# Features on partitions: conv inputs, memory queries and tile 1's gate and up without turns, with the norm's factor spread

## The chip, the cores and the metric

The kernel runs on one core of a Trainium2 chip, in one launch. The metric is the device time of that launch in microseconds. TensorE (PE in the profile) multiplies, VectorE (DVE) and ScalarE (ACT) work element by element, GpSimd (POOL) issues the gathers, SyncE (SP) issues the weight transfers. All numbers are 32-bit floats. A matmul of 32-bit operands stands in the trace as two records, each with its own weight load; a turn (a transpose through PE against the identity) is one record.

## The reference, cut to what matters

There are 256 tokens of 1024 features. A first block (retention and differential attention, then a feed-forward that gathers 128 experts for each token) ends in x; a second block of two layers runs on it. What the change touches is in the second block:

```python
h = rms_norm_2(x, norm_mix[0])                     # x * rsqrt(mean(x*x) + eps) * g
b_gate, c_gate, u = jnp.split(h @ w_in, 3, axis=-1)       # short_conv_mixer, 1024 x 3072
z = c_gate * u
conv = causal depthwise convolution of z over 3 tokens
x = x + (b_gate * conv) @ w_out

q = rms_norm_2(x, norm_mem[l]) @ w_q               # mem_cross_attention, both layers
s = einsum(q, k) * 256 ** -0.5; p = softmax(s)
x = x + merge(p @ v) @ w_o

g, u = jnp.split(rms_norm_2(x, norm_ffn[l]) @ w_gu, 2, axis=-1)   # swiglu, 1024 x 5632
x = x + (jax.nn.silu(g) * u) @ w_down
```

## The kernel before, in words

**Tiles and units.** The tokens are two tiles of 128 (tile 0 and tile 1). A product of the second block is cut into units: one unit is 1024 input features by 512 output columns (a 2 MB piece of weights), or 128 tokens by 512 columns of output, and fills one PSUM bank. Four banks (`bank[u % 4]`) go round in the order of the list `UNITS`; a unit opens when the unit four before it has been read by its engine (D for DVE, A for ACT). `layer_unit` (L954 to L965) does one with eight matmuls of 128x512: the stationary operand is a block of the input `hT` (features on partitions, 128 tokens as columns), the moving operand is the weight piece in the ring, and the result has tokens on partitions. The norm's gain is put on while `x` is turned (step `turn`); the norm's factor `rs`, one number for each token, is found meanwhile (squares, mean, step `root` with the square root, reciprocal) and put on as the unit is read, where it is a scalar for each partition.

**Turns.** The next product needs features on partitions again, so results are turned in blocks of 128x128 (`layer_turns`, L972), four to a bank. Steps `zturn` and `bturn` turn the conv's z and gate (8 blocks each), `qturn` the memory queries (8 blocks in each layer), `fturn` the 22 blocks of silu(gate) times up (in each layer, six steps). Then come `cout`, `scores` and `dn`.

**Two phases.** First the rows phase: PE, DVE, ACT and POOL go in pairs through 256 expert picks. POOL gathers for each pick 128 rows of 8 KB (1 MB, L1601) into one of 8 slots; the gather of pick n may start when the V rows of pick n-8 have been used by PE. DVE makes the dots (L2063), in order; ACT the gelu and a diagonal (L1546 to L1559); PE adds the V rows with four matmuls for each pair (L1128, eight records). The layer steps of tile 0 run between these pairs: `PICK_WORK[n]` says which steps stand ahead of pair n. A small planner sets this: for each step it has a cost in us and a lag in picks (`STEPS`); a step starts no earlier than the one before it plus the lag, and the load moves on by cost / 5.2. On PE the steps of pick n come ahead of the matmuls of pair n; ACT and DVE do them two picks later in their own order. By the planner tile 0's first step stands at pick 138 and its last one in this phase, `fturn1 5`, at pick 252.

Then the tail: all steps of tile 1 (`AFTER_ROWS`), with the six `dn1` units and the last norm of tile 0 put between them as fill.

**Weights.** SP loads the pieces in the order of use (L587) into a ring, of which three slots serve the second block; a slot is loaded again when its unit is done. Each tile loads its pieces anew.

Of the kernel before, what the change touches and what calls it, by code (L numbers as in the profile page):

```python
# [202 lines left out]
def feed_steps(l):  # L203

    steps = [(f"turn ffn{l}", 2, 2), (f"root ffn{l}", 0, 0)]
    for j in range(11):
        steps.append((f"gu{l} {j}", 7, 0 if j else 2))
        if j >= 2 and j % 2 == 0:
            steps.append((f"fturn{l} {j // 2 - 1}", 1, 0))
    return steps + [(f"fturn{l} 5", 1, 2)] + [(f"dn{l} {c}", 7, 0 if c else 2) for c in range(6)]  # L210


STEPS = ([("turn conv", 2, 2), ("root conv", 0, 0), ("cin 2", 7, 2), ("cin 4", 7, 0), ("cin 3", 7, 0), ("cin 5", 7, 0), ("cin 0", 7, 0), ("zturn 0", 2, 0),
          ("taps 0", 0, 0), ("cin 1", 7, 0), ("bturn 0", 2, 2), ("cout 0", 7, 2), ("cout 1", 7, 0)] + memory_steps(0) + feed_steps(0)
         + [("turn blk", 2, 2), ("root blk", 0, 0), ("bk 0", 7, 2), ("bk 1", 7, 0), ("bq 0", 7, 0), ("bq 1", 7, 0), ("bv 0", 7, 0), ("rope 0", 0, 0),
            ("bv 1", 7, 0), ("kturn 0", 2, 2), ("bqturn 0", 2, 0), ("bscores 0", 2, 2), ("bprobs 0", 0, 2), ("bpturn 0", 2, 2), ("bvalues 0", 3, 2),
            ("bo 0", 7, 2), ("bo 1", 7, 0)] + memory_steps(1) + feed_steps(1) + [("final 0", 0, 2)])
# [3 lines left out]
for _w, _us, _lag in STEPS:  # L221
# [9 lines left out]
for _w, _us, _lag in STEPS:  # L231
# [4 lines left out]
def units_of(work):  # L236
# [18 lines left out]
    if kind == "layer":  # L255
# [3 lines left out]
                {"turn": [("t{a}{t}0", "D"), ("t{a}{t}1", "A")], "cin": [("ci{t}{a}", "D" if arg in "45" else "A")], "zturn": [("z{t}0", "D"), ("z{t}1", "A")],  # L259
# [27 lines left out]

def unit(name):
    return [n for n, _ in UNITS].index(name)
# [21 lines left out]
TileBuffers = namedtuple("TileBuffers", """squares hT kvT b_tok z_tok q_tok zT cvT qT oT probs probs_low pT sg f_tok fT fT4 k_tok bq_tok kq rot v_tok kT  # L311
# [5 lines left out]
def build_program(nc, a, out):  # L317
# [5 lines left out]
    with ExitStack() as ctx:  # L323
# [97 lines left out]
        def tile_buffers(t):  # L421
# [12 lines left out]
            if t:  # L434
                fT = [arena[:, k * P:(k + 1) * P] for k in range(FC)]
                fT4 = [arena[:, 512 * m:512 * m + 512] for m in range(6)]
            heads = 8 * (t + 1)
# [5 lines left out]
                sg=[v[:, 0:512].rearrange("p (b n) -> p b n", b=2) for v in (first, later)], f_tok=[v[:, 512:1024] for v in (first, later)], fT=fT, fT4=fT4,  # L443
# [68 lines left out]
        tile_max, tile_probs, tile_silu = ([sem(f"tile{t}_{n}") for t in range(NT)] for n in ("max", "probs", "silu"))  # L512
        block_max, block_exp, block_probs = ([sem(f"tile{t}_block_{n}") for t in range(NT)] for n in ("max", "exp", "probs"))
# [82 lines left out]
        def _(pe):  # L596
# [360 lines left out]
            def layer_unit(name, piece_of, src, low, high):  # L957
# [3 lines left out]
                b = open_unit(name)  # L961
                for k in range(KC):
                    if k == 4:
                        unit_read(high)
                    m = mm(b[:, :], src[:, k], slot8[w][:, k], start=(k == 0), stop=(k == KC - 1))  # L965
# [9 lines left out]
            def layer_step(t, step, arg):  # L975
# [7 lines left out]
                elif kind == "cin":  # L983
                    layer_unit(f"ci{t}{arg}", (f"cin{t}", int(arg)), v.hT, f"tconv{t}0", f"tconv{t}1")
                elif kind == "zturn":
                    for u in range(2):
                        unit_read(f"ci{t}{4 + u}")
                        layer_turns(f"z{t}{u}", [v.z_tok[:, (4 * u + c) * P:(4 * u + c + 1) * P] for c in range(4)])
                elif kind == "bturn":
                    for u in range(2):  # L990
                        unit_read(f"ci{t}{u}")
                        layer_turns(f"b{t}{u}", [v.b_tok[:, (4 * u + c) * P:(4 * u + c + 1) * P] for c in range(4)])
                elif kind == "cout":
                    layer_unit(f"co{t}{arg}", (f"cout{t}", int(arg)), v.cvT, f"b{t}0", f"b{t}1")
                elif kind == "q":
                    layer_unit(f"lq{l}{t}{arg}", (f"q{l}{t}", int(arg)), v.hT, f"tmem{l}{t}0", f"tmem{l}{t}1")
                elif kind == "qturn":
                    for u in range(2):
                        unit_read(f"lq{l}{t}{u}")
                        layer_turns(f"qt{l}{t}{u}", [v.q_tok[:, (4 * u + c) * P:(4 * u + c + 1) * P] for c in range(4)])  # L1000
                elif kind == "scores":
                    K = feat(mem[2 * l])
                    unit_read(f"mk{l}11")
                    for i in range(2):
                        unit_read(f"qt{l}{t}{i}")
# [23 lines left out]
                elif kind == "gu":  # L1029
                    layer_unit(f"gu{l}{t}{arg}", (f"gu{l}{t}", int(arg)), v.hT, f"tffn{l}{t}0", f"tffn{l}{t}1")  # L1030
# [4 lines left out]
                elif kind == "dn":  # L1035
# [4 lines left out]
                    for k in ks:  # L1040
                        if half == 0 and k % 4 == 0:
# [111 lines left out]
        def _(act):  # L1153
# [275 lines left out]
            def layer_step(t, step, arg):  # L1429
# [8 lines left out]

                if kind == "turn":
# [27 lines left out]
                elif kind == "cin":  # L1467
                    i, ss, ms, sd, rs = tile_stats(t, "conv")
                    c = int(arg)
                    if c < 4:  # L1470
                        scaled(f"ci{t}{c}", (v.b_tok if c < 2 else v.z_tok)[:, (c % 2) * 512:(c % 2 + 1) * 512])
                elif kind == "zturn":
                    unit_copy(f"z{t}1", v.zT[:, 4:8, 2:2 + P])
                elif kind == "taps":
                    act.wait_ge(unit_free["D"], units_freed(f"z{t}0", "D"))
                    act.wait_ge(unit_free["A"], units_freed(f"z{t}1", "A"))
                    for c in range(KC):
                        f(v.cvT[:, c], v.zT[:, c, 0:P], ACT.Copy, scale=cols[:, C_CONV + c:C_CONV + c + 1]).then_inc(sem("tap0"), 1)
                elif kind == "q":
                    i, ss, ms, sd, rs = tile_stats(t, f"mem{l}")  # L1480
                    scaled(f"lq{l}{t}{arg}", v.q_tok[:, int(arg) * 512:(int(arg) + 1) * 512])
                elif kind == "qturn":
                    unit_copy(f"qt{l}{t}1", v.qT[:, 4:8])
                elif kind == "scores":
                    for i in range(2):
# [121 lines left out]
        def _(dve):  # L1607
# [504 lines left out]
            def layer_step(t, step, arg):  # L2112
# [11 lines left out]
                elif kind == "root":  # L2124
                    i, ss, ms, sd, rs = tile_stats(t, arg)
                    dve.wait_ge(tile_root[t], i + 1)
                    nc.vector.reciprocal(rs, sd).then_inc(tile_rs[t], 1)
                elif kind == "final":
# [14 lines left out]
                    ts(high, high, rs, None, ALU.mult).then_inc(sem(f"tile{t}_done1"), 1)  # L2143
                elif kind == "cin" and arg in "45":
                    i, ss, ms, sd, rs = tile_stats(t, "conv")
                    u = int(arg) - 4
                    copied(f"ci{t}{2 + u}")
                    dve.wait_ge(tile_rs[t], i + 1)
                    part = v.z_tok[:, u * 512:(u + 1) * 512]
# [174 lines left out]
```

## Time and profile before

| | us |
|---|---|
| three timed runs | 1788.23, 1793.31, 1794.34 (median 1793.31) |
| the profiled execution | 1786.05 |
| its span in the trace | 1784.2 |
| PE busy | 1606.3 (90% of the span), 5460 matmul records |
| weight loads on PE | 748.9 (42%) |
| DVE, ACT, POOL busy | 751.5, 501.2, 281.2 |
| bytes moved | 595.22 MB, mean 334 GB/s |

Matmul records overlap: each stands with its own latency in it, and its neighbour starts before it ends. The pace of PE is read from the distance between starts. Windows are in us from the span's start; the rows phase ends and the tail begins near 1296.

### The profile page before, as it was taken

What the parts mean: (1) busy time and instruction counts of PE and PEld (TensorE: products, weight loads), DVE (VectorE), ACT (ScalarE), POOL (GpSimd) and SP (SyncE); (2) the same over time, 40 slices, a digit from 0 to 9 for tenths busy, and PEclk for the clock granted to TensorE, in tenths of its full rate; (3) what the DMA queues carried; (4) which work ended last, traced back from release to release, by engine and by line L of the source; (5) the groups of instructions that cost most, each with busy time, mean ns of one, the idle gap of its engine ahead of it and who ended that gap; (6) DMA issues with size and microseconds to landing.
All of it is one profiled execution on the core that took longest, in us unless ns stands there. A gap on an engine that the chain in (4) does not pass through costs nothing.

```text
span 1784.2 us, 15530 instructions
## 1 busy us (share of the span) xinstructions
PE 1606.3 (90%) x5460; PEld 748.9 (42%) x5460; DVE 751.5 (42%) x1808; ACT 501.2 (28%) x1283; POOL 281.2 (16%) x268
## 2 busy tenths in 40 slices
PE   6998988588659998699899997999999999999998
PEld 3444455154115353244344333343344544455443
DVE  3653036866586556655543446542212100031101
ACT  3311123322232223423344233334411210122210
POOL 1000001323232433412211222231100000000000
PEclk9998999799889999899999998999999999999999
DMA  9545146999999999999999999999977677765774
GB/s 355 197 171 189 78 194 259 404 376 414 422 413 359 395 422 421 421 414 417 404 422 421 420 421 422 395 422 421 409 272 265 236 295 286 302 236 224 282 286 185
DMA packets 94957, 595.22 MB, mean 334 GB/s; under 512 B 7024, under 2 KB 7024, under 8 KB 28192
## 3 DMA queue, kind: packets, MB, share of 16 engines
q1 hardware_dynamic: 56576, 319.28, 45.8%
q0 software_dynamic: 37584, 270.75, 37.0%
q10 hardware_dynamic: 720, 4.19, 0.6%
q8 instruction: 44, 0.72, 0.2%
q14 instruction: 33, 0.27, 0.0%
HBM read 593.15 MB, written 1.05 MB: 333 GB/s over the span
## 4 chain that ended last, share of the span: by engine, by line
PE 77%; DMA 13%; DVE 6%; ACT 2%; issue 2%; POOL 1%; SPq 0%; POOLq 0%; DVEq 0%; ACTq 0%
PE bank L965 35%; PE bank L1128 9%; DMA arena<-in_peer_rows,pidx 8%; PE bank L1043 8%; PE bank L675 7%; PE bank L937 3%; PE bank L928 3%; PE bank L752 3%; DMA ring<-in_w_mod 2%; PE bank L972 2%; DMA ring<-in_weights 2%; DVE arena L2063 1%; PE bank L729 1%; PE bank L1025 1%; PE bank L647 1%
## 5 line engine op out<-in xcount | busy, mean ns | idle before, releaser
L1601 POOL DMA_INDIRECT arena<-in_peer_rows,pidx x256 | 276.4, 1080 | 968.4 <-PE bank L1128 647.5
L2063 DVE SCALAR_TENSOR_TENSOR arena<-arena,ring 128x1024 f32<-128x1024 f32 x256 | 306.1, 1222 | 152.5 <-DMA arena<-in_peer_rows,pidx 151.3
L1128 PE MATMUL bank<-arena,keep 128*32 128x512 f32 x1024 | 266.2, 664 | 93.2 <-ACT keep L1559 93.1
L965 PE MATMUL bank<-ring,arena 128*128 128x512 f32 x736 | 319.4, 593 | 0.0
L965 PE MATMUL bank<-ring,hT_all 128*128 128x512 f32 x544 | 241.0, 599 | 3.4 <-issue 3.4
L965 PEld LDWEIGHTS bank<-ring,arena 128*128 128x128 f32 x736 | 138.5, 190 | 168.8 <-issue 168.7
L1128 PEld LDWEIGHTS bank<-arena,keep 128*32 128x32 f32 x1024 | 51.2, 116 | 257.2 <-issue 128.5
L965 PEld LDWEIGHTS bank<-ring,hT_all 128*128 128x128 f32 x544 | 101.8, 191 | 135.7 <-issue 135.7
L1546 ACT ACTIVATE pf<-pf 128x2 f32<-128x2 f32 x128 | 25.8, 202 | 374.7 <-DVE arena L2063 368.3
L2179 DVE TENSOR_TENSOR x_all<-x_all,bank 128x512 f32<-128x512 f32 x40 | 27.5, 688 | 202.5 <-PE bank L1043 107.4
L675 PE MATMUL bank<-ring,hT_all 128*128 128x512 f32 x192 | 89.3, 624 | 3.0 <-DVE hT_all L1678 3.0
L1043 PE MATMUL bank<-ring,arena 128*128 128x512 f32 x176 | 75.9, 592 | 0.0
L1559 ACT ACTIVATE keep<-keep,pf 128x32 f32<-128x32 f32 x256 | 68.3, 313 | 4.2
L2202 DVE SCALAR_TENSOR_TENSOR arena<-bank,stat,arena 128x256 f32<-128x256 f32 x22 | 10.6, 484 | 137.1 <-ACT arena L1502 137.1
L1552 ACT ACTIVATE pf<-pf,grouped 128x1 f32<-128x1 f32 x256 | 61.4, 287 | 4.2
L752 PE MATMUL bank<-hT_all,ring 128*128 128x128 f32 (+1 forms) x384 | 60.3, 317 | 0.3 <-ACT hT_all L1163 0.3
L675 PEld LDWEIGHTS bank<-ring,hT_all 128*128 128x128 f32 x192 | 38.0, 201 | 51.6 <-issue 51.6
L752 PEld LDWEIGHTS bank<-hT_all,ring 128*128 128x128 f32 x384 | 54.9, 197 | 8.8 <-issue 5.6
L928 PE MATMUL bank<-mem_all,ring 128*128 128x256 f32 x256 | 57.3, 382 | 0.0
L1043 PE MATMUL bank<-ring,s_all 128*128 128x512 f32 x128 | 56.5, 596 | 0.6 <-DMA ring<-in_weights 0.6
L937 PE MATMUL bank<-ring,mem_all 128*128 128x512 f32 x128 | 57.0, 598 | 0.0
L965 PE MATMUL bank<-ring,s_all 128*128 128x512 f32 x128 | 56.0, 595 | 0.8 <-issue 0.8
(374 smaller groups left out, 1561.8 us busy)
## 6 DMA issues: line engine op xcount, KB each, us to landing
ring<-in_weights SPq DMA_DIRECT2D x126, 2048.0 KB
ring<-in_w_mod SPq DMA_DIRECT2D x12, 2048.0 KB
ring<-in_w_in SPq DMA_DIRECT2D x6, 2048.0 KB
ring<-in_weights SPq DMA_DIRECT2D x8, 1024.0 KB
arena<-in_peer_rows,pidx POOLq DMA_INDIRECT x256
ring<-in_weights SPq DMA_DIRECT2D x8, 512.0 KB
mem_all<-in_b_mod POOLq DMA_DIRECT2D x3, 512.0 KB, 9.6
hT_all<-in_xT ACTq DMA_DIRECT2D x1, 1024.0 KB, 6.6
```

What stands on the lines that cost most here:

```text
L675: m = mm(b[:, :], src[:, k, t * P:(t + 1) * P], slot8[w][:, k], start=(k == 0), stop=(k == KC - 1))
L752: m = mm(b[:, s * n:(s + 1) * n], slot8[w][:, k, c:c + P], hT[:, k, cols_of], start=(k == 0), stop=(k == KC - 1))
L928: m = mm(bk[:, b * TOK:(b + 1) * TOK], slot8[w][:, k, (2 * half + b) * P:(2 * half + b + 1) * P], memT[l][:, k], start=(k == 0), stop=(k = ...
L937: m = mm(b[:, :], memT[l][:, k, t * P:(t + 1) * P], slot4[w][:, k % 4, half * 512:(half + 1) * 512], start=(k == 0), stop=(k == KC - 1))
L965: m = mm(b[:, :], src[:, k], slot8[w][:, k], start=(k == 0), stop=(k == KC - 1))
L972: i = tr(b[:, c * P:(c + 1) * P], src, ident)
L1043: m = mm(b[:, :], v.fT[k], slot8[w][:, k % 8], start=(k == ks[0]), stop=(k == ks[-1]))
L1128: m = mm(acc[b][r:r + 32, :], diag[n % 8], vslot[n % SLOTS][:, b * 512:(b + 1) * 512], start=(n % 128 < 4), stop=(n % 128 >= 124))
L1552: m = f(pw2[:, c + k:c + k + 1], pgel2[:, c + k:c + k + 1], ACT.Copy, scale=grouped[:, g % 4, i % 4, 1, i // 4:i // 4 + 1])
L1559: f(diag[n % 8], eq32, ACT.Copy, scale=pw2[:, c + k:c + k + 1]).then_inc(sem("diag_ready"), 1)
L1601: nc.gpsimd.indirect_dma_start(out=row_in[n % SLOTS], out_offset=None, in_=a["peer_rows"], in_offset=bass.IndirectOffsetOnAxis(ap=pidx[:, ...
L2063: stt(uslot[n % SLOTS], uslot[n % SLOTS], 1.0, h2g[n % 4], ALU.mult, ALU.mult, accum_out=pact2[:, 16 * (g % 2) + k:16 * (g % 2) + k + 1]). ...
```

## The change

The named units are computed the other way round. `turned_unit` takes 128 columns of the weight piece as the stationary operand and the 128 tokens of `hT` as the moving one: 32 matmuls of 128x128 instead of 8 of 128x512. The result has features on partitions, in four blocks to a bank, and needs no turn. This is done for the six `cin` and the two `q` units of each layer in both tiles, and for the 22 `gu` units in tile 1 alone (`TURNED_FEED`). The steps `zturn`, `bturn` and `qturn` go, and tile 1's `fturn`.

The norm's factor now runs along the free axis, and is not put on at the same place. For the conv and for tile 1's feed-forward DVE writes a diagonal matrix of `rs`, PE multiplies it with a matrix of ones (step `spread`, one matmul of 128x128), and ACT copies the result, which holds the factor of each token in all partitions (`rows`). For the conv its square goes on z (both factors at once) and the gate's factor goes on after `cout`. For the feed-forward it goes on the gate half ahead of silu, and the up half's factor goes on after `dn`. For the memory queries it goes into the scale of the exponential. The adds of `cout` and of tile 1's `dn` become one operation with the factor in it.

```diff
-    return [(f"turn mem{l}", 2, 2), (f"root mem{l}", 0, 0), (f"q{l} 0", 7, 2), (f"q{l} 1", 7, 0), (f"qturn{l} 0", 2, 2), (f"scores{l} 0", 4, 2),
+    return [(f"turn mem{l}", 2, 2), (f"root mem{l}", 0, 0), (f"q{l} 0", 7, 2), (f"q{l} 1", 7, 0), (f"scores{l} 0", 4, 2),
...
+TURNED_FEED = (1,)
...
+        if t in TURNED_FEED and j == 0:
+            steps.append((f"spread ffn{l}", 0, 0))
+        if t not in TURNED_FEED and j >= 2 and j % 2 == 0:
             steps.append((f"fturn{l} {j // 2 - 1}", 1, 0))
...
-STEPS = ([("turn conv", 2, 2), ("root conv", 0, 0), ("cin 2", 7, 2), ("cin 4", 7, 0), ("cin 3", 7, 0), ("cin 5", 7, 0), ("cin 0", 7, 0), ("zturn 0", 2, 0),
-          ("taps 0", 0, 0), ("cin 1", 7, 0), ("bturn 0", 2, 2), ("cout 0", 7, 2), ("cout 1", 7, 0)] + memory_steps(0) + feed_steps(0)
+STEPS = [[("turn conv", 2, 2), ("root conv", 0, 0), ("cin 2", 7, 2), ("spread conv", 0, 0), ("cin 4", 7, 0), ("cin 3", 7, 0), ("cin 5", 7, 0), ("cin 0", 7, 0),
+          ("taps 0", 0, 0), ("cin 1", 7, 0), ("gate 0", 0, 0), ("cout 0", 7, 2), ("cout 1", 7, 0)] + memory_steps(0) + feed_steps(t, 0)
...
+            def turned_unit(name, piece_of, src, low, high):
 
                 w = weights(piece[piece_of])
                 unit_read(low)
                 b = open_unit(name)
+                for half in range(2):
+                    if half:
+                        unit_read(high)
+                    for c in range(4):
+                        for k in range(4 * half, 4 * half + 4):
+                            m = mm(b[:, c * P:(c + 1) * P], slot8[w][:, k, c * P:(c + 1) * P], src[:, k], start=(c == k == 0), stop=(c == 3 and k == KC - 1))
+                m.then_inc(unit_ready, 1)
...
+                elif kind == "spread":
+                    pe.wait_ge(tile_diag[t], spreads(t, arg) + 1)
+                    b = open_unit(f"rb{arg}{t}")
+                    mm(b[:, 0:P], v.ones[arg == "ffn1"], v.diag[arg == "ffn1"], start=True, stop=True).then_inc(unit_ready, 1)
...
-                        if half == 0 and k % 4 == 0:
+                        if half == 0 and t in TURNED_FEED and k % 2 == 0:
+                            unit_read(f"gu{l}{t}{k // 2}")
...
-                              scale=MSCALE, accum_out=zz[:, h:h + 1])
+                              scale=scale, accum_out=zz[:, h:h + 1])
...
+                    if t in TURNED_FEED:
+                        if j == 0:
+                            spread_copy(f"ffn{l}")
+                        act.wait_ge(tile_gained[t], 11 * l + j + 1)
+                        f(v.sg[l][:, j % 2], v.sg[l][:, j % 2], ACT.Silu).then_inc(tile_silu[t], 1)
+                        return
...
+                    if arg == "conv" or arg[:3] == "ffn" and t in TURNED_FEED:
+                        dve.wait_ge(tile_rs[t], i + 1)
+                        ts(v.diag[arg == "ffn1"], ident, rs, None, ALU.mult).then_inc(tile_diag[t], 1)
...
+                    link(tt(part, part, v.rows2.unsqueeze(1).to_broadcast([P, 4, P]), ALU.mult))
+                    tt(v.zT[:, 4 * u:4 * u + 4, 2:2 + P], unit_in(f"ci{t}{arg}")[:, :].rearrange("p (c n) -> p c n", c=4), part, ALU.mult).then_inc(unit_free["D"], 1)
...
+                elif kind == "gate":
                     for u in range(2):
+                        copied(f"ci{t}{u}")
+                        tt(v.cvT[:, 4 * u:4 * u + 4], v.cvT[:, 4 * u:4 * u + 4], v.b_tok[:, u * 512:(u + 1) * 512].rearrange("p (c n) -> p c n", c=4),
+                           ALU.mult).then_inc(tile_gated[t], 1)
...
+                        stt(x[:, t, c], unit_in(name)[:, :], rs, x[:, t, c], ALU.mult, ALU.add).then_inc(unit_free["D"], 1)
...
+                        tt(sg, part[:, 0:2], v.rows[l].unsqueeze(1).to_broadcast([P, 2, P]), ALU.mult).then_inc(tile_gained[t], 1)
+                        dve.wait_ge(tile_silu[t], 11 * l + j + 1)
+                        tt(v.fT2[j], part[:, 2:4], sg, ALU.mult).then_inc(unit_free["D"], 1)
+                        return
```

## Rows read from the trace of the kernel before

**Rows 1.** The page: DMA share over the span in 40 slices.

```profile
DMA  9545146999999999999999999999977677765774
```

**Rows 2.** Windows: us, busy PE, PEld, DVE, ACT, POOL, PEclk, DMA share, GB/s.

```profile
738.00:1296.00 558.00, 523.95 (x1614) 216.05 (x1616) 259.34 (x617) 206.41 (x518) 123.28 (x115) 0.97 1.01 416
...
1240.00:1296.00 56.00, 55.80 (x164) 21.65 (x164) 17.09 (x31) 25.32 (x51) 8.97 (x8) 1.00 1.00 412
...
1296.00:1784.00 488.00, 474.45 (x1336) 228.09 (x1332) 76.04 (x170) 80.03 (x169) 0.00 (x0) 1.00 0.69 260
```

**Rows 3.** Waits, 738 to 1296: us in total, times, longest.

```profile
DVE arena L2063 <- DMA arena<-in_peer_rows,pidx: 47.3, 26, 4.3
...
PE bank L1128 <- ACT keep L1559: 9.3, 5, 4.0
```

**Rows 4.** Timeline of PE, turns and their neighbours in the tail: start, us, what.

```profile
1345.71 1.04 PE L972 MATMUL bank<-keep,arena 128*128 128x128 f32 x8
1346.59 7.03 PE L965 MATMUL bank<-ring,arena 128*128 128x512 f32 x16
1353.45 0.60 PE L972 MATMUL bank<-keep,arena 128*128 128x128 f32 x4
...
1354.95 1.52 PE L965 MATMUL bank<-ring,arena 128*128 128x512 f32 x3
...
1384.16 0.60 PE L972 MATMUL bank<-keep,arena 128*128 128x128 f32 x4
...
1385.60 3.69 PE L1009 MATMUL bank<-mem_all,arena 128*128 128x256 f32 x16
...
1435.57 0.60 PE L972 MATMUL bank<-keep,arena 128*128 128x128 f32 x4
1436.01 13.90 PE L965 MATMUL bank<-ring,arena 128*128 128x512 f32 x32
...
1492.26 0.60 PE L972 MATMUL bank<-keep,arena 128*128 128x128 f32 x4
...
1494.12 2.31 PE L1043 MATMUL bank<-ring,arena 128*128 128x512 f32 x5
...
1737.60 0.60 PE L972 MATMUL bank<-keep,arena 128*128 128x128 f32 x4
...
1739.12 2.31 PE L1043 MATMUL bank<-ring,arena 128*128 128x512 f32 x5
```

**Rows 5.** Timeline of PE, runs of 128-column matmuls.

```profile
385.04 3.74 PE L752 MATMUL bank<-hT_all,ring 128*128 128x128 f32 x32
...
1395.93 3.81 PE L1025 MATMUL bank<-arena,mem_all 128*128 128x128 f32 x32 [0.62 <-ACT arena L1176]
```

**Rows 6.** Groups by line: busy us, mean ns, idle before.

```profile
L2150 DVE SCALAR_TENSOR_TENSOR arena<-bank,stat,arena 128x512 f32<-128x512 f32 x2 | 1.5, 750 | 26.1 <-PE bank L965 26.1
...
L1025 PEld LDWEIGHTS bank<-arena,mem_all 128*128 128x128 f32 x64 | 7.3, 192 | 1.7 <-issue 1.7
```

**Rows 7.** Timeline of DVE and ACT: second feed-forward's norm factor, one silu.

```profile
1663.35 0.16 DVE L2127 RECIPROCAL stat<-stat 128x1 f32<-128x1 f32 x1 [2.39 <-ACT stat L1453]
...
1667.38 0.47 ACT L1502 ACTIVATE arena<-bank,stat 128x256 f32<-128x256 f32 x1 [2.50 <-PE bank L965]
```

**Rows 8.** Timeline of PE, the last pairs of the rows phase.

```profile
1271.87 1.91 PE L1128 MATMUL bank<-arena,keep 128*32 128x512 f32 x8
...
1294.83 1.91 PE L1128 MATMUL bank<-arena,keep 128*32 128x512 f32 x8 [0.20 <-ACT keep L1559]
```

**Rows 9.** Timeline of POOL, gathers issued.

```profile
1158.22 1.24 POOL L1601 DMA_INDIRECT arena<-in_peer_rows,pidx  x1 [0.30 <-issue]
...
1275.79 1.11 POOL L1601 DMA_INDIRECT arena<-in_peer_rows,pidx  x1 [0.30 <-issue]
```

**Rows 10.** Timeline of DVE, dots of the rows that those gathers bring.

```profile
1167.07 1.22 DVE L2063 SCALAR_TENSOR_TENSOR arena<-arena,ring 128x1024 f32<-128x1024 f32 x1 [1.26 <-DMA arena<-in_peer_rows,pidx]
...
1292.23 1.22 DVE L2063 SCALAR_TENSOR_TENSOR arena<-arena,ring 128x1024 f32<-128x1024 f32 x1
```

More of the change, by code:

```diff
@@ L258, in units_of @@
         return [(n.format(t=t, a=arg, s=step, l=step[-1]), e) for n, e in
-                {"turn": [("t{a}{t}0", "D"), ("t{a}{t}1", "A")], "cin": [("ci{t}{a}", "D" if arg in "45" else "A")], "zturn": [("z{t}0", "D"), ("z{t}1", "A")],
[2 rows of a table removed]
+                {"turn": [("t{a}{t}0", "D"), ("t{a}{t}1", "A")], "cin": [("ci{t}{a}", "D" if arg in "45" else "A")], "spread": [("rb{a}{t}", "A")], "cout": [("co{t}{a}", "D")], "q": [("lq{l}{t}{a}", "A")],
+                 "scores": [("sc{l}{t}0", "A"), ("sc{l}{t}1", "A")],
                  "pturn": [("pt{l}{t}0", "D"), ("pt{l}{t}1", "A")], "values": [("v{l}{t}0", "D"), ("v{l}{t}1", "A")],
@@ L442, in tile_buffers @@
                 pT=work.rearrange("p (h k n) -> p h k n", h=MH, k=2),
-                sg=[v[:, 0:512].rearrange("p (b n) -> p b n", b=2) for v in (first, later)], f_tok=[v[:, 512:1024] for v in (first, later)], fT=fT, fT4=fT4,
+                sg=[v[:, 0:512].rearrange("p (b n) -> p b n", b=2) for v in (first, later)], f_tok=[v[:, 512:1024] for v in (first, later)], fT=fT, fT4=fT4, fT2=fT2,
+                ones=[b[:, 0:P] for b in spare], diag=[b[:, P:2 * P] for b in spare], rows=[b[:, 2 * P:3 * P] for b in spare], rows2=spare[0][:, 3 * P:4 * P],
                 k_tok=low, bq_tok=high, kq=both.rearrange("p (g n) -> p g n", g=16), rot=work[:, 0:512].rearrange("p (s g n) -> p s g n", s=2, g=16),
@@ L512, in build_program @@
         tile_max, tile_probs, tile_silu = ([sem(f"tile{t}_{n}") for t in range(NT)] for n in ("max", "probs", "silu"))
+        tile_diag, tile_gated, tile_gained = ([sem(f"tile{t}_{n}") for t in range(NT)] for n in ("diag", "gated", "gained"))
         block_max, block_exp, block_probs = ([sem(f"tile{t}_block_{n}") for t in range(NT)] for n in ("max", "exp", "probs"))
@@ L961, in layer_unit @@
                 b = open_unit(name)
+                for half in range(2):
[5 more added lines that the diff above has]
+                m.then_inc(unit_ready, 1)
+            def layer_unit(name, piece_of, src, low, high, t=None):
+                w = weights(piece[piece_of])
+                if t is None:
+                    unit_read(low)
+                else:
+                    pe.wait_ge(tile_gated[t], 1)
+                b = open_unit(name)
                 for k in range(KC):
-                    if k == 4:
+                    if k == 4 and t is None:
                         unit_read(high)
+                    elif k == 4:
+                        pe.wait_ge(tile_gated[t], 2)
                     m = mm(b[:, :], src[:, k], slot8[w][:, k], start=(k == 0), stop=(k == KC - 1))
@@ L983, in layer_step @@
                 elif kind == "cin":
[L984 to L992, printed above, removed]
+                    turned_unit(f"ci{t}{arg}", (f"cin{t}", int(arg)), v.hT, f"tconv{t}0", f"tconv{t}1")
+                elif kind == "spread":
+                    pe.wait_ge(tile_diag[t], spreads(t, arg) + 1)
+                    b = open_unit(f"rb{arg}{t}")
+                    mm(b[:, 0:P], v.ones[arg == "ffn1"], v.diag[arg == "ffn1"], start=True, stop=True).then_inc(unit_ready, 1)
                 elif kind == "cout":
-                    layer_unit(f"co{t}{arg}", (f"cout{t}", int(arg)), v.cvT, f"b{t}0", f"b{t}1")
+                    layer_unit(f"co{t}{arg}", (f"cout{t}", int(arg)), v.cvT, None, None, t)
                 elif kind == "q":
[L996 to L1000, printed above, removed]
+                    turned_unit(f"lq{l}{t}{arg}", (f"q{l}{t}", int(arg)), v.hT, f"tmem{l}{t}0", f"tmem{l}{t}1")
                 elif kind == "scores":
@@ L1040, in layer_step @@
                     for k in ks:
-                        if half == 0 and k % 4 == 0:
+                        if half == 0 and t in TURNED_FEED and k % 2 == 0:
+                            unit_read(f"gu{l}{t}{k // 2}")
+                        elif half == 0 and t not in TURNED_FEED and k % 4 == 0:
                             unit_read(f"ft{l}{t}{k // 4}")
@@ L1437, in scaled, with spread_copy @@
                     f(dst, bank[unit(name) % 4][:, :], ACT.Copy, scale=rs).then_inc(unit_free["A"], 1)
+                def spread_copy(norm):
+                    name = f"rb{norm}{t}"
+                    act.wait_ge(unit_ready, unit(name) + 1)
+                    f(v.rows[norm == "ffn1"], bank[unit(name) % 4][:, 0:P], ACT.Copy).then_inc(unit_free["A"], 1)
                 if kind == "turn":
```

84 lines of the change are left out of this document (44 added, 40 removed), and 2 rows, old and new, of the table late.

## The prediction

> **What bounds the kernel now.** I read the DMA share on the page first. From the seventh slice to the thirtieth it stands at 9: until the last expert row is in, the transfers hardly pause; behind that they fall to 6 or 7 [rows 1]. The table by stage says the same in numbers [rows 2]. While tile 0's layers run among the picks (738 to 1296) DMA is busy throughout at 416 GB/s, and PE is busy for 524 of 558 us. In the tail (1296 to 1784) DMA has room, 260 GB/s at 0.69, and PE is busy for 474 of 488 us at the full clock. So the tail is PE's alone: what PE no longer issues there comes off the end, and what it issues more is added. In the rows phase two bounds lie on each other. The waits say how closely: DVE, which makes the dots in order, stood 47.3 us over 26 times for rows that had not landed, but only 9.3 us of it went through to PE [rows 3]. In the last 56 us of this phase PE hardly stops at all, 55.8 us busy, and DMA is full too [rows 2]. A step moved in this phase can therefore cost as well as save.
>
> **The tail: what goes.** PE runs the tail in a fixed order, so what a group of turns costs is the distance from its first start to the start of what follows, waits included [rows 4]. `zturn`: 1346.59 - 1345.71 = 0.88. `bturn`: 1354.95 - 1353.45 = 1.50, of which about 0.6 is a wait for ACT's copy of the last unit. `qturn`: 1385.60 - 1384.16 = 1.44, in layer 1 the same to 0.01, so 2.88. `fturn` between units: 1436.01 - 1435.57 = 0.44, four in each layer, 3.52. The last two `fturn` steps of a layer stand behind the last `gu` unit and wait for silu and DVE: 1494.12 - 1492.26 = 1.86 and 1739.12 - 1737.60 = 1.52. Sum 12.16 us.
>
> Is something late in their place? `cout 0` needs the first gated half at its start, and its fifth matmul, 3.4 us in, the second: a copy and one DVE product of at most 0.75 each [rows 6], some 1.7 us after `cin 1`. Covered, as long as the taps are done during `cin 0` and `cin 1`, 14 us. `scores` begins on the first query half, and PE spends half of the 3.5 us that the scores take [rows 4] before it needs the second, whose copy takes under 1 us. `dn 0` starts on blocks of `gu 0` and meets those of `gu 10` only in the third unit, 14 us on. I take no new wait in any of the three. If the cover failed, each would cost what the wait in its old turn cost, 0.5 to 1.4 us.
>
> **The tail: what comes.** 32 units are turned round in tile 1 (6 `cin`, 4 `q`, 22 `gu`). A unit as before takes 1353.45 - 1346.59 = 6.86 us for its 16 records, 0.429 each [rows 4]. A turned unit is 64 records of 128 columns, each with its own weight load. The trace has such runs. Queries of the first block take their stationary operand from the ring just as the new units do, and 32 records last 3.74 us [rows 5]. The last one shows its latency too: four turns last 0.60 where the next start comes after 0.44 [rows 4], so 0.16 or 0.17 is overlap. (3.74 - 0.17) / 32 = 0.1116, and 64 of them are 7.14 us, 0.28 more than before. The run in the tail, 3.81 us [rows 5], gives 0.1138 and 0.42. I take 0.29, since the first row has the operand in the same place: 32 x 0.29 = 9.3 us. The bounds are 0 (a quarter of 0.429 for each) and 13.4. The three `spread` matmuls are two records each with a gap, 0.3 each, 0.9; their factor is there in time: in layer 1 the reciprocal starts at 1663.35, and with a diagonal behind it (one 128x128 product, under 0.75) it is ready before `gu 0`, which starts some 3 us ahead of it, has run its 7.1 us [rows 7]. Bounds 0.2 and 1.5 each time.
>
> DVE and ACT get work for each `gu` unit: two DVE products of 128x256 around a silu of 0.47 [rows 7], at most 2 us, with PE 7.1 us in every unit and four banks between them. That costs nothing; it would take over 7 us for each unit to show. The add behind `cout` and `dn` becomes the operation with the factor, 0.75 us for 128x512 [rows 6]; three times PE or the end waits for it, 0.06 to 0.1 longer each, together 0.2.
>
> The tail: -12.16 + 9.3 + 0.9 + 0.2 = **-1.8 us**, between -11 (turned units for nothing) and +6.
>
> **The rows phase: what PE does.** In tile 0 32 turns go, about 0.44 for four, -3.5; ten units are turned round, +2.9; one spread, +0.3. That is -0.3, nothing. `gu` stays as it was there.
>
> **The rows phase: what moves.** Here lies the larger term. `qturn` held two picks in each layer (lag 2), so everything behind it moves up: `scores0` from pick 158 to 156, `gu1 10` from 250 to 246, the last `fturn1 5` from 252 to 248. The picks stay where they are, so four pairs (248, 250, 252, 254) now stand behind all big layer work and not two. Follow the end. Before, from pair 246 at 1271.87 to pair 254 at 1294.83 [rows 8] were 22.96 us, and PE spent it on four pairs, `gu1 9` and `gu1 10`. Now between the same pairs are only four pairs of 1.9 us and two turns, 8 us. But pair 254 needs rows 254 and 255, whose slots come free with pair 246. Row 255 was issued at 1275.79, 3.9 us after pair 246 began [rows 8, 9]; its dot began at 1292.23, and PE's pair followed 2.6 us later [rows 8, 10], so 6.5 us lie around the transfer. The transfer: row 255's dot stood 16.4 us behind its issue, but PE's own work held DVE back then. The gather issued at 1158.22 had its dot at 1167.07, and that one waited for DMA and nothing else: 8.85 us [rows 9, 10]. So from pair 246 to pair 254 it takes 6.5 + 8.85 = 15.4 us at least with such a transfer, 22.9 at most, where PE has work for 8.
>
> When does pair 246 begin? `gu1 10` ends with two pairs fewer ahead of it, -3.7, and -0.3 from above: pair 246 takes the place that pair 250 had (22.96 less 4.3 for pairs 250 and 252 behind it, so 18.65 us after 1271.87, at 1290.5), now at 1286.5. If transfers had set the pace until then, four rows fewer (4.2 MB at 416 GB/s, 10 us) would have brought it up to 1280.5. Pair 254 then begins at 1286.5 + 15.4 = 1301.9 instead of 1294.8, **+7.1**; in the early case at 1295.9, +1.1; with the early case and no wait at all -6; with the slow transfer +14.6. PE was busy for 55.8 of the last 56 us [rows 2], which speaks for the late start; four rows fewer in the queue speak for a little of the other. I take **+5**. The cost is a wait: PE idle ahead of the last pairs, with nothing of the tail moved into it, because the tail's steps stand behind pair 254 in PE's order.
>
> **Sum.** -1.8 + 5 = +3.2 us on the profiled execution's 1786.05 us (span 1784.2 and 1.9 around it): 1789.2. That execution is 7.3 us under the median of the three timed runs, 1793.31. The difference is carried over to the median: 1796.5.
>
> **The rivals.**
>
> *The transfers keep the rows phase, and four rows fewer pay.* For it: DVE's 47.3 us of waits for rows [rows 3]. Each step of the layers is reached with up to 4.2 MB less to be moved, and if the backlog is worked off ahead of the end, pair 254 comes with the last byte, some 4 us before its old time. Against it: the last rows can't be asked for before pair 246. -1.8 - 4 - 2 (waits of PE for rows that vanish, of its 9.3) = -8: 1785.
>
> *The end of the rows phase is slow.* The other side: one mechanism, rows 252 to 255. They queue with the weight piece that the slot of `gu1 10` asks for at the same moment, and take the 16.4 us that row 255 stood before. Pair 254 comes 14 us late, and as PE idles its clock may fall to 1.2 GHz for some us, where it was at 0.97 of full over this phase and at full in the last 56 us [rows 2]: +1.5. -1.8 + 14 + 1.5 = +13.7: 1807. It decides from the point at which 246 to 254 takes over 17 us.
>
> *The weight loads show.* If 128 columns don't cover a weight load of 0.192 us [rows 6], a turned unit takes 64 x 0.192 = 12.3 us, 5.4 more; 32 units in the tail +174, ten in tile 0 +54: 2021. Against it stand both runs of rows 5, at 0.112 and 0.114 for a record. The Trainium skill speaks for this one (TensorE: Matmul & The Clock Gate, section Back-to-back issue gap): it gives a sustained 81 ns for a matmul of 128 columns and 131 ns for one of 512, so that four narrow ones cost 2.5 times a wide one; by that, as an estimate, a turned unit would take 17 us and the tail would grow by some 320 us. The trace does not agree: 4 x 0.1116 against 0.429 is a factor of 1.04, so the measurement decides.
>
> **How the numbers follow.** Forecast 0.5, the transfers' gain 0.2, the slow end 0.27, the weight loads 0.03. What a measurement of this kernel can tell from no change is 0.3%, 5.4 us. The forecast, +3.2, lies inside, so: faster 0.2, within 0.5, slower 0.3. The forecast's own range is 1791 to 1801 (the tail -5 to +1, the end of the rows phase +1 to +8). To hold 8 in 10 the range goes down to the transfers' gain and up to just under the slow end's 1807: 1785 to 1806.
>
> **What the profile after would show.** The tail from its first `dn1` unit to the last one shorter by 1 to 3 us, no L972 records between `gu` units of tile 1, and runs of 64 records in 7.1 to 7.3 us. In the rows phase: from pair 246 to pair 254 15 us or more in place of 22.96, of which 7 or more are PE idle, put down to ACT's diagonal and behind it to a gather; the tail's start near 1302. It would be wrong if that stretch had no idle time (then the first rival), or if a turned unit took over 7.6 us, or if `cout`, `scores` or `dn 0` began with a wait.

## The result and the profile after

| | before | after |
|---|---|---|
| median of 15 timed runs, us | 1789.22 (1782.80 to 1795.73) | 1796.13 (1791.46 to 1800.68) |
| span of the profiled execution, us | 1784.2 | 1792.2 |
| from the first tail unit to the end, us | 487.6 | 485.1 |
| matmul records | 5460 | 7376 |

The changed kernel is slower: ratio 1.0036, 95% interval 1.0023 to 1.0049, which is 6.4 us (4 to 9). In the two profiled executions the spans differ by 8.0 us: 10.5 are lost before the tail begins and 2.5 are won in it.

The page of the changed kernel, the DMA share in 40 slices, and beneath it its windows by stage (the columns of [rows 2]):

```profile
DMA  9545246999999999999999999999957687866785
```

```profile
738.00:1307.00 569.00, 525.01 (x2066) 256.30 (x2066) 259.38 (x621) 204.38 (x514) 120.80 (x114) 0.96 0.99 408
1240.00:1307.00 67.00, 56.28 (x166) 19.96 (x163) 19.26 (x34) 24.75 (x54) 11.39 (x10) 0.92 0.89 370
1307.00:1792.00 485.00, 473.85 (x2800) 352.52 (x2798) 85.91 (x198) 71.28 (x157) 0.00 (x0) 1.00 0.72 261
```

PE is busy for the same time as before among the picks (525.0 against 523.95) and in the tail (473.9 against 474.5) [rows 2]. What is new stands in the middle line: in the last 67 us of the rows phase PE idles for 10.7 us, and DMA, which was full before, is at 0.89. The 0.89 is a mean of two stretches. From 1283 to 1298, the larger part of PE's wait included, the DMA engines are full; they fall idle only when the last rows are nearly in, and then PE alone works through what is left:

```profile
1283.00:1298.00 15.00, 7.68 (x35) 2.06 (x35) 5.24 (x9) 5.02 (x14) 2.01 (x2) 0.84 1.01 422
1299.00:1307.00 8.00, 4.60 (x12) 0.56 (x8) 2.18 (x4) 1.22 (x5) 0.00 (x0) 0.72 0.03 13
```

The end of the rows phase on PE, which answers to [rows 8]: two `fturn` groups, the five pairs 246, 248, 250, 252 and 254, and the start of the tail's first unit.

```profile
1283.09 0.60 PE L1005 MATMUL bank<-keep,s_all 128*128 128x128 f32 x4
1283.62 1.91 PE L1155 MATMUL bank<-arena,keep 128*32 128x512 f32 x8
1285.46 0.44 PE L1005 MATMUL bank<-keep,s_all 128*128 128x128 f32 x2
1285.83 1.91 PE L1155 MATMUL bank<-arena,keep 128*32 128x512 f32 x8
1287.94 1.91 PE L1155 MATMUL bank<-arena,keep 128*32 128x512 f32 x8 [0.20 <-ACT keep L1593]
1296.96 3.42 PE L1155 MATMUL bank<-arena,keep 128*32 128x512 f32 x8 [7.12 <-ACT keep L1593]
1303.78 3.42 PE L1155 MATMUL bank<-arena,keep 128*32 128x512 f32 x8 [3.40 <-ACT keep L1593]
1307.13 1.12 PE L1070 MATMUL bank<-ring,s_all 128*128 128x512 f32 x2
```

The waits of 7.12 and 3.40 us name ACT's diagonal. What ACT waited for is in the chain of waits through the same place (start, us, what), which leads back over the dot to a gather:

```profile
1283.69 1.89 PE bank L1155 x8
...
1286.30 1.07 POOL arena L1635
...
1287.67 13.48 DMA arena<-in_peer_rows,pidx
...
1301.18 1.25 DVE arena L2097 x2
...
1303.20 0.54 ACT keep L1593 x2
...
1303.78 3.42 PE bank L1155 x8
```

Pair 246 lets the slot go. The last gather is issued 4 us after that pair began and takes 13.5 us; dot, gelu and diagonal take 2.6. The two late pairs last 3.42 us each and not 1.91: PE had idled before them, and the clock granted over the first of them was 1.2 GHz, half of 2.4 (PEclk 0.50 in the window below). The first one's 1.5 us lies in the wait of the second; the second one's is added.

```profile
1297.00:1300.00 3.00, 3.00 (x8) 0.52 (x8) 1.23 (x2) 0.00 (x0) 0.00 (x0) 0.50 0.57 238
```

In the tail, a timeline of PE from the first conv unit to `cout`. 64 records to a turned unit, two for the spread, and then `cout` without a wait:

```profile
1321.85 7.31 PE L982 MATMUL bank<-arena,ring 128*128 128x128 f32 x64
1328.99 0.39 PE L1021 MATMUL bank<-arena 128*128 128x128 f32 x2
1329.21 35.90 PE L982 MATMUL bank<-arena,ring 128*128 128x128 f32 x320
1364.95 2.31 PE L998 MATMUL bank<-ring,arena 128*128 128x512 f32 x5
```

Five units last 35.74 us, 7.15 each where the old form takes 6.86 [rows 4]. The spread takes 0.22. None of the places where turns stood has a wait: PE goes straight from `cin 1` to `cout`, from the queries to the scores, and from the last `gu` unit to `dn`.

### The profile page after: what moved, and what is told of

Read it like the earlier page. It is cut to its first block, busy times and chain, and to the rows that moved or that the text cites. A ratio compares the mean times of both kernels' runs of the same rounds, so it can differ in the third digit from the quotient of the medians.

```text
span 1792.2 us, 19299 instructions
## 1 busy us (share of the span) xinstructions
PE 1611.6 (90%) x7376; PEld 913.6 (51%) x7376; DVE 762.2 (43%) x1840; ACT 490.9 (27%) x1269; POOL 279.2 (16%) x268
## 4 chain that ended last, share of the span: by engine, by line
PE 76%; DMA 14%; DVE 6%; ACT 2%; issue 2%; POOL 1%; POOLq 0%; SPq 0%; DVEq 0%; ACTq 0%
PE bank L998 19%; PE bank L982 16%; PE bank L1155 9%; DMA arena<-in_peer_rows,pidx 9%; PE bank L1070 8%; PE bank L690 7%; PE bank L952 3%; DMA ring<-in_w_mod 3%; PE bank L767 2%; PE bank L943 2%; DMA ring<-in_weights 2%; DVE arena L2097 2%; PE bank L1005 1%; PE bank L744 1%; PE bank L662 1%
## 5 line engine op out<-in xcount | busy, mean ns | idle before, releaser
L982 PE MATMUL bank<-arena,ring 128*128 128x128 f32 x2048 | 230.3, 275 | 0.0
L982 PEld LDWEIGHTS bank<-arena,ring 128*128 128x128 f32 x2048 | 229.4, 192 | 1.3 <-issue 1.3
L998 PE MATMUL bank<-ring,hT_all 128*128 128x512 f32 x384 | 169.2, 595 | 0.9 <-issue 0.9
L998 PEld LDWEIGHTS bank<-ring,hT_all 128*128 128x128 f32 x384 | 71.3, 190 | 92.4 <-issue 92.4
L998 PE MATMUL bank<-ring,arena 128*128 128x512 f32 x224 | 97.0, 592 | 0.0
L690 PE MATMUL bank<-ring,hT_all 128*128 128x512 f32 x192 | 89.4, 624 | 3.0 <-DVE hT_all L1712 3.0
L1070 PE MATMUL bank<-ring,arena 128*128 128x512 f32 x176 | 75.9, 592 | 0.0
L982 PEld LDWEIGHTS bank<-hT_all,ring 128*128 128x128 f32 x640 | 72.0, 192 | 4.8 <-issue 4.8
L982 PE MATMUL bank<-hT_all,ring 128*128 128x128 f32 x640 | 73.1, 276 | 0.5 <-issue 0.5
L998 PEld LDWEIGHTS bank<-ring,arena 128*128 128x128 f32 x224 | 42.3, 190 | 51.7 <-issue 51.7
L2221 DVE TENSOR_TENSOR x_all<-x_all,bank 128x512 f32<-128x512 f32 x24 | 16.5, 687 | 114.0 <-PE bank L998 74.6
L690 PEld LDWEIGHTS bank<-ring,hT_all 128*128 128x128 f32 x192 | 38.1, 201 | 51.7 <-issue 51.7
L1203 ACT ACTIVATE arena<-bank 128x512 f32<-128x512 f32 x30 | 17.9, 597 | 160.3 <-PE bank L982 66.2
```

Of the source, the lines that this page charges most:

```text
L690: m = mm(b[:, :], src[:, k, t * P:(t + 1) * P], slot8[w][:, k], start=(k == 0), stop=(k == KC - 1))
L982: m = mm(b[:, c * P:(c + 1) * P], slot8[w][:, k, c * P:(c + 1) * P], src[:, k], start=(c == k == 0), stop=(c == 3 and k == KC - 1))
L1070: m = mm(b[:, :], v.fT[k], slot8[w][:, k % 8], start=(k == ks[0]), stop=(k == ks[-1]))
```

## The experiments

Nine more kernels were run, five rounds each beside the kernel before the change. Stretch, start and length of the tail are in us and come from one profiled execution of each kernel; the stretch is the time from the start of pair 246 to the start of pair 254 on PE.

| kernel | ratio to before (95%) | stretch | tail begins | tail |
|---|---|---|---|---|
| before | 1 | 22.96 | 1296.7 | 487.6 |
| changed | 1.0036 (1.0023 to 1.0049) | 20.16 | 1307.1 | 485.1 |
| early4 | 1.0062 (1.0040 to 1.0084) | 19.44 | 1304.4 | 487.7 |
| late4 | 0.9997 (0.9983 to 1.0012) | 22.96 | 1303.0 | 485.1 |
| late2 | 1.0012 (0.9994 to 1.0031) | 20.83 | 1305.3 | 485.1 |
| pace5 | 1.0018 (1.0001 to 1.0034) | 21.16 | 1307.9 | 485.4 |
| after_last4_out | 0.9958 (0.9941 to 0.9974) | 8.90 | 1295.2 | 485.1 |
| before_last4_out | 0.9989 (0.9973 to 1.0005) | 22.96 | 1295.7 | 487.6 |
| dn0_in_rows | 1.0022 (1.0007 to 1.0038) | 25.27 | 1313.4 | 479.7 |
| nofeed_late4 | 0.9990 (0.9972 to 1.0009) | 22.96 | 1301.2 | 484.9 |
| tile1_only | 1.0003 (0.9986 to 1.0019) | 22.96 | 1298.9 | 485.1 |

The tail of the changed kernel stands in six traces, and lasts 485.1 us in five of them; in pace5 it is 485.4, as PE is still slow at its start (the first unit lasts 7.51 us instead of 7.13). Whole times spread more: the 15 executions of the changed kernel lie within 9 us, the 15 of the one before within 13. So tails and stretches are compared by the profiles, whole times by the ratios. An interval reaches 2 to 4 us to either side of its ratio, and two versions whose ratios differ by less than about 4 us are not told apart by them. The start of a tail is that of one execution.

**late4.** The old places, the new units.

```diff
-    ... (f"scores{l} 0", 4, 2),
+    ... (f"scores{l} 0", 4, 4),
```

> The changed kernel, with the lag of the scores step raised from 2 to 4 picks in both layers, so that tile 0's steps stand at the same picks as before the change (last fturn1 5 at pick 252). Theory (the loss is the end of the rows phase, the tail gained 2.5 us): the stretch from pair 246 to pair 254 goes back from 20.2 to 23 us with under 1 us of PE idle, the tail begins near 1296 instead of 1307, the tail stays at 485 us; in all 2 to 4 us faster than the kernel before the change, 9 to 11 faster than the changed one. Rival A (the turned conv and query units or the new waits cost the time in the rows phase): the tail begins near 1303 to 1307 all the same and the time stays within 2 us of the changed kernel, 6 us slower than before.

```profile
1296.87 1.91 PE L1155 MATMUL bank<-arena,keep 128*32 128x512 f32 x8
1298.71 0.44 PE L1005 MATMUL bank<-keep,s_all 128*128 128x128 f32 x2
1299.08 1.91 PE L1155 MATMUL bank<-arena,keep 128*32 128x512 f32 x8
1301.19 1.91 PE L1155 MATMUL bank<-arena,keep 128*32 128x512 f32 x8 [0.20 <-ACT keep L1593]
```

The timeline of PE shows the last three pairs as they were before, with 0.2 us of idle time. The loss is gone: 1.0036 falls to 0.9997. But 2 to 4 us under before were expected, and it is level. The tail has its 2.5 us; it begins at 1303.0, though. The theory expected 1296, Rival A 1303 to 1307. By the whole time Rival A is wrong; by the start of the tail it may be right in part, and tile1_only goes back to that.

**early4.** The old units, the new places: in the kernel before, the lag of scores from 2 to 0.

> The kernel before the change, with the lag of scores taken from 2 picks to 0, so that tile 0's steps behind the scores stand 2 and then 4 picks earlier, as in the changed kernel, and no unit is turned round. Theory: PE waits 7 to 12 us for rows ahead of the last pairs, the tail begins 8 to 12 us later (near 1305 to 1308), the tail stays 487.5 us; 8 to 12 us slower than before. One or two us of it are the scores waiting for the copies of qturn just ahead of them. Rival A (the turned units cost the time): within 2 us of before.

It came out 0.62% slower, 11 us (7 to 15), with none of the turned units in it. Its timeline has the same two waits:

```profile
1293.06 3.63 PE L1128 MATMUL bank<-arena,keep 128*32 128x512 f32 x8 [5.48 <-ACT keep L1559]
1300.80 3.63 PE L1128 MATMUL bank<-arena,keep 128*32 128x512 f32 x8 [4.11 <-ACT keep L1559]
```

So the move alone is enough. The two places where the scores now stand right behind `qturn` cost little: PE waits 0.4 us at each. With those 0.8 us and the 2.5 us of the tail taken off, 11.1 becomes 7.8, which agrees with the measured 6.4 within the intervals.

**after_last4_out and before_last4_out.** The gathers of the last four picks are left out, in the changed kernel and in the one before.

```diff
-            for n in range(16 * PK):
+            for n in range(16 * PK - 4):
...
-                    dve.wait_ge(rows_in[n % SLOTS], 16 * (n // SLOTS + 1))
+                    if n < 252:
+                        dve.wait_ge(rows_in[n % SLOTS], 16 * (n // SLOTS + 1))
```

> The changed kernel without the gathers of the last four picks (252 to 255): their dots and products run on what lies in the slots, so that part of the result is left out; all instructions of PE, DVE and ACT and all layer weights stay. Theory (PE stands before pairs 252 and 254 for the landing of those rows): the two waits of 7.1 and 3.4 us go, but for up to 2 us of the chain dot, gelu, diagonal; from pair 246 to pair 254 it takes 8.5 to 11 us instead of 20.2, the tail begins 9 to 12 us earlier, the time is 9 to 12 us under the changed kernel, 2 to 5 under the one before. Rival (the chain over DVE and ACT with its table loads is what PE waits for): it stays above 16 us and the time moves by less than 4.

> The same left out of the kernel before the change (gathers of picks 252 to 255). There gu1 9 and gu1 10 stand behind pair 246 and hide those rows: theory 22.96 us from pair 246 to pair 254 as with the gathers, less at most 0.2, and a time within 2 us of before. Rival (the bytes of the rows phase as a whole set its end, 4.2 MB at 416 GB/s): 5 to 10 us faster than before.

```profile
1288.78 1.91 PE L1155 MATMUL bank<-arena,keep 128*32 128x512 f32 x8 [0.20 <-ACT keep L1593]
1291.07 1.91 PE L1155 MATMUL bank<-arena,keep 128*32 128x512 f32 x8 [0.38 <-ACT keep L1593]
1293.36 1.91 PE L1155 MATMUL bank<-arena,keep 128*32 128x512 f32 x8 [0.38 <-ACT keep L1593]
```

In the changed kernel (PE's timeline above) both waits and the low clock go, the stretch falls from 20.16 to 8.90 us, the tail begins 11.9 us sooner, and the ratio falls by 0.0078, 14 us, somewhat more than the 9 to 12 expected. The chain over DVE and ACT leaves 0.38 us a pair. In the kernel before, leaving out the same four gathers gives 0.9989, 2 us that are not told from nothing, and the stretch is unchanged to the hundredth. The same rows are free in one order and cost over 10 us in the other; this pair of runs settles the cause of the loss at the end of the rows phase.

**late2 and pace5.** Two other ways to move the steps back: two picks in layer 1 only, and a planner that reckons 5.0 us for a pick.

```diff
-    ... (f"scores{l} 0", 4, 2),
+    ... (f"scores{l} 0", 4, 2 + 2 * l),
```

```diff
-LAYER_FIRST, PICK_US = 136, 5.2
+LAYER_FIRST, PICK_US = 136, 5.0
```

> The changed kernel with two picks of lag given back in layer 1 only, so that its last layer step stands at pick 250 (248 in the changed kernel, 252 before it), and three pairs stand behind the last big unit instead of four. Theory (rows 252 to 255 set the last pairs): from pair 246 to pair 254 is gu1 10 (6.9 us) and four pairs and turns, 16 us of work against 19 to 21 for the rows, so 3 to 5 us of PE idle instead of 10.5; 3 to 5 us faster than the changed kernel, 1 to 3 slower than late4. Rival (a threshold: four pairs or nothing): equal to late4.

> The changed kernel with the planner's pace at 5.0 us for a pick instead of 5.2 and no lag changed: the steps stand up to four picks later towards the end (turn ffn1 at 232, gu1 10 at 248, last fturn1 5 at 252), spread over dn0 and gu1 instead of as gaps behind the queries. Theory (the end decides, wherever the picks were gained): the idle time of 10.5 us ahead of the last pairs goes to under 3, the time is that of late4 within 2 us, 5 to 9 faster than the changed kernel. If gaps behind the queries cost rows waits, it is 1 to 3 us better than late4. Rival (late4 gained by its gaps behind the queries, not by the end): no better than the changed kernel.

late2 lies between, as expected: by the ratios 4 us under the changed kernel and 3 over late4, by its trace 5.5 us idle. The ratios alone would not tell it from late4; the idle time does. pace5 missed. Its last step stands at pick 252 as in late4, yet PE waits 5.6 us, and it came out 4 us slower than that one, again at the edge of the intervals. The reason is in its timeline:

```profile
1283.66 1.91 PE L1155 MATMUL bank<-arena,keep 128*32 128x512 f32 x8
1285.50 7.13 PE L998 MATMUL bank<-ring,hT_all 128*128 128x512 f32 x16
1292.57 1.91 PE L1155 MATMUL bank<-arena,keep 128*32 128x512 f32 x8
...
1299.31 1.91 PE L1155 MATMUL bank<-arena,keep 128*32 128x512 f32 x8 [2.04 <-ACT keep L1593]
1304.82 3.18 PE L1155 MATMUL bank<-arena,keep 128*32 128x512 f32 x8 [3.60 <-ACT keep L1593]
```

`gu1 10`, the last large unit, stands at pick 248 here, as in late2, and both lose alike. What counts is not where the last step stands but how much of the layer work lies behind the pair that frees the last slots: two large units (late4, nothing lost), one (5 to 6 us idle) or none (10.5). That holds for units left in their order; dn0_in_rows, next, puts a unit of the tail there, and PE idles as long as with none.

**dn0_in_rows.** Fill the hole instead: tile 0's first `dn1` unit from the tail to pick 250.

```diff
-UNDER_ROWS, DOWN = [], [f"dn1 {c}" for c in range(6)]
+UNDER_ROWS, DOWN = [], [f"dn1 {c}" for c in range(1, 6)]
...
-FILLS = {"turn conv": ["dn1 0"], "cin 2": ["dn1 1"], "pturn0 0": ["dn1 2"], "bk 0": ["dn1 3"], ...
+FILLS = {"turn conv": ["dn1 1"], "pturn0 0": ["dn1 2"], "bk 0": ["dn1 3"], ...
```

> The changed kernel, with tile 0's unit dn1 0 moved from the tail to the rows phase (pick 250), where PE stood idle for 10.5 us; the fill dn1 1 takes its place ahead of turn conv, dn1 2 to 5 go to the four places that hide a softmax or an add, and the place ahead of cin 2 has none. Theory: the last rows still set the last pairs, so the tail begins at 1305 to 1308 as in the changed kernel, and is 6.9 us shorter less under 1 us of new wait at cin 2: 478 to 479 us. 5 to 7 us faster than the changed kernel, about level with before (0 to 1 faster). Rival (the idle stretch is set by PE's order, not by rows): the tail begins 6.9 us later and nothing is gained.

```profile
1288.59 7.13 PE L1070 MATMUL bank<-ring,s_all 128*128 128x512 f32 x16
1295.66 1.91 PE L1155 MATMUL bank<-arena,keep 128*32 128x512 f32 x8
1299.57 1.91 PE L1155 MATMUL bank<-arena,keep 128*32 128x512 f32 x8 [2.00 <-ACT keep L1593]
1309.81 3.63 PE L1155 MATMUL bank<-arena,keep 128*32 128x512 f32 x8 [8.33 <-ACT keep L1593]
```

The tail, now without this unit, is 5.4 us shorter than in the changed kernel, near the 6.1 to 7.1 expected, but it begins at 1313.4, where 1305 to 1308 were expected. By the ratios 2.5 us come through, which the intervals don't tell from nothing, and 5 to 7 were expected: this missed. The rival's numbers (6.9 us later, nothing gained) fit better than the theory's; its mechanism doesn't, for the waits still lead back to rows: the unit runs in the hole, behind it PE waits 10.3 us again, and DVE's four waits for rows at this end add up to 15.4 us where they were 10.9.

The traces say what the theory left out. When the unit ends, its ring slot is free, and SP asks for the next 2 MB of weights while the last rows are still on their way. These are SP's issues from 1268 to 1314, in dn0_in_rows, where the third comes right behind the unit, near 1296, and then in the changed kernel:

```profile
1275.30 20.84 SPq L602 DMA_DIRECT2D ring<-in_weights  x3
```

```profile
1274.38 9.29 SPq L602 DMA_DIRECT2D ring<-in_weights  x2
```

Between pair 246 and the dot of row 255 the rows' queue moved 3.8 MB in both kernels, the weights' queue 4.63 MB here and 2.57 in the changed one, and the DMA engines were full up to 1304 (1.01, 419 GB/s). 2.06 MB at 419 GB/s are 4.9 us, as an estimate; pair 254 came 5.1 us later behind pair 246 than in the changed kernel. So what hides the last rows must not itself ask for bytes ahead of them. A run that holds this one piece back was not made.

**nofeed_late4.** late4 with `TURNED_FEED = ()`: tile 1's gate and up as before.

> As late4, and TURNED_FEED empty: tile 1's gate and up as before the change, with fturn, only conv inputs and queries turned round. By the rows of both traces, in the tail turning the 22 gate-up units costs 22 x 0.28 + 2 x 0.22 = 6.6 us and the fturn steps gave back 6.9, so this part is worth 0.3 us and nothing that can be measured: expected equal to late4 within 1 us, the tail at 485 to 486. Rival B (the gain in the tail comes from the feed-forward, whose last fturn waits go): 3 us slower than late4, level with before.

Level with late4, tail 484.9 against 485.1, so Rival B is wrong. Turning round 22 of the 32 units in the tail is worth nothing: each adds 0.28 us, and together they eat up what the turns and waits they replace had cost.

**tile1_only.** Tile 0 gets back its old conv and query steps (both paths stand in the kernel, chosen by tile); tile 1 is as changed.

> The change in tile 1 alone: tile 0 keeps its conv and query units with tokens on partitions, zturn, bturn and qturn, and with them its places at the picks (last fturn1 5 at 252). late4 had those places too, but its rows phase came out some microseconds longer than before the change, as DVE waited 58 us for rows where it had waited 47. Theory: between the picks PE only hands time to the waits for rows, so tile 0's turns cost nothing there; with tile 0 as before, the rows phase is that of the kernel before (tail begins at its place, 1296 to 1300 in the profile) and the tail has 485.1 us: 2 to 3 us faster than before, 1 to 3 faster than late4. Rival (the excess of late4 was the luck of one execution): level with late4 within 1 us, level with before within 1.

The ratios, 1.0003 here and 0.9997 for late4, tell neither from before nor from each other; 2.5 us, 0.14%, lies inside both intervals, and the 2 to 3 us under before that were expected did not show. The profiles say more. DVE's waits for rows and PE's waits for the diagonal, 738 to 1305, in late4 and then in tile1_only (us, times, longest), to be read against the 47.3 and 9.3 of [rows 3]:

```profile
DVE arena L2097 <- DMA arena<-in_peer_rows,pidx: 58.0, 29, 4.7
...
PE bank L1155 <- ACT keep L1593: 16.2, 5, 7.6
```

```profile
DVE arena L2137 <- DMA arena<-in_peer_rows,pidx: 45.7, 25, 4.0
...
PE bank L1180 <- ACT keep L1633: 10.8, 5, 4.9
```

nofeed_late4, the second kernel with late4's tile 0, has 59.8 and 16.8. DVE's sum goes with the form of tile 0's units and not with their places: it is 58 to 66 us in the six kernels with tile 0 turned and all rows gathered, and 42 to 47 in the three without (before, tile1_only, early4). It reaches PE in late4 and nofeed_late4 above all, where PE no longer has `qturn` between the first pairs behind the queries: from 850 to 872 it stands for 12.6 and 11.8 us, against 8.7 before the change and 8.3 in tile1_only. That fits a rows phase in which transfers set the pace wherever no large unit stands. How much of late4's later start is this and how much the spread between executions stays open; in the ratios none of it shows. No version that computes the whole result beat the kernel before by more than its uncertainty.

## Why the prediction was right, and where it was off

*The time.* 1796.5 was forecast, 1796.13 measured, inside the range of 1785 to 1806. That the two are so close is luck: two misses cancelled. The three runs shown had a median of 1793.31, fifteen have 1789.22, so the base was 4 us too high; the change forecast was +3.2 us, the measured one +6.4, so the change was undersized by half. It fell just beyond 0.3%, into the "slower" that had 0.3, not into the likeliest "within" (the interval, 0.23 to 0.49%, reaches over both).

*The tail* was forecast at -1.8 and measured at -2.5. The terms: 12.16 us of turns and waits gone, as listed, with no new wait at `cout`, `scores` or `dn 0`; 32 x 0.283 = 9.1 for the turned units (9.3 forecast); three spreads at 0.22, 0.7 (0.9); the longer adds 0.2, which no run measured by itself. These give -2.2; where the other 0.3 us went was not traced.

*The rows phase* was the larger term with the right sign and mechanism, and this is the step that was mis-sized: "I take +5" for pair 254, which came 8.95 us late. Three numbers went into it. Pair 246 was put at 1286.5 or, if transfers had set the pace, at 1280.5; it came at 1283.6, between. Around the transfer 6.5 us were taken, and 6.7 measured. The transfer itself was taken at 8.85 us, the shortest one seen, and took 13.48. It was issued 1.4 us behind another gather, with weights under way and the DMA engines full (1.01 from 1283 to 1298), and the shortest time does not hold there. The bound from the other side, 16.4, was nearer, and the middle of the two, 12.6, would have given +8 with pair 246 where it came. On top, the last two pairs ran at 1.2 GHz, which moves the tail's start to +10.5; this stood only in the rival of the slow end, at 1.5 us, its measured size, and the forecast put it at nothing.

*The rivals.* The transfers' gain did not come: pair 246 was 2.9 us ahead of its late estimate, but the last rows could not be asked for earlier, as the text said against it. The slow end had the measured mechanism, the late landing beside weights and the low clock, at too high a price; the outcome, a stretch of 20.2 us, is past its own point of decision, 17 us, and between it (+13.7) and the forecast. So of the two it is this rival whose mechanism was met. The weight loads stayed hidden in all 42 turned units: their records start 0.112 to 0.113 us apart.

*What the text had wrong in kind.* It counted the pairs behind the last big unit and the step `fturn1 5`, as if both measured the same thing. pace5 shows that they don't. It took the last rows' time from when their slots come free alone; dn0_in_rows shows that the bytes asked for ahead of them count as much. And one reading was off, with nothing resting on it: in [rows 1] the 9s run from the eighth slice to the twenty-ninth, not from the seventh to the thirtieth.

## What to carry to other kernels

Where work stands in a hand-written order against a stream of transfers with a fixed number of slots, removing a step also moves everything behind it; before taking out a step, follow the last transfers of the stream and ask what work is left to hide them, and which other bytes that work asks for ahead of them. Removing operations from an engine that shares its bound with the transfers gives the time to the waits; only where that engine is alone on the path (the tail here) does it come off. Turning a product round to save a transpose trades a fixed cost for each unit against the turns: with ten conv and query units in place of 32 turns and three waits it gained, with 22 gate-up units in place of 44 turns and two waits it gave nothing.

## What the runs showed of the hardware

A matmul record of 128 columns with its own 128x128 weight load keeps a pace of 0.1117 us over 320 records in a row, where the load alone stands in the trace with 0.192 us; the same columns in one record of 512 take 0.429. With the DMA engines full, the last gathers took 13.5 us in the changed kernel, and with another 2 MB of weights asked for ahead of them pair 254 came 5.1 us later still (dn0_in_rows).

Behind waits of 3.4 to 8.3 us at the end of the rows phase eight records that take 1.91 us took 3.2 to 3.6, with a granted clock of 0.50 over the first such group of the changed kernel; behind waits of 2 us there (pace5, dn0_in_rows) they took 1.91 as before. The length of the last wait does not decide it, as the changed kernel's timeline shows further ahead, where a wait of 2.07 us has a slow group behind it and one of two equal waits a fast group:

```profile
401.79 3.14 PE L1155 MATMUL bank<-arena,keep 128*32 128x512 f32 x8 [2.07 <-ACT keep L1593]
...
554.18 1.91 PE L1155 MATMUL bank<-arena,keep 128*32 128x512 f32 x8 [3.15 <-ACT keep L1593]
...
744.82 3.62 PE L1155 MATMUL bank<-arena,keep 128*32 128x512 f32 x8 [3.15 <-ACT keep L1593]
```
